# Tokens into the state in matmuls of 128 rows: four token phases side by side, picked out by selection matmuls, and powers of B and C computed 1024 wide

## The reference, cut to what matters

```python
def _s5_mixer(u, a_re, a_im, log_dt, b_re, b_im, c_re, c_im, d, w_glu):
    uf = u.reshape(bsz, L, SSM_GROUPS, SSM_GROUP).astype(f32)       # 256 tokens, 64 groups of 16
    dt = jnp.exp(log_dt)[:, None]
    mag, ang = jnp.exp(a_re * dt), a_im * dt
    lb_re, lb_im = mag * jnp.cos(ang), mag * jnp.sin(ang)            # the eigenvalue lambda
    ...
    bb_re = f_re[..., None] * b_re - f_im[..., None] * b_im          # B, scaled by a complex factor f
    bb_im = f_re[..., None] * b_im + f_im[..., None] * b_re
    bu_re = jnp.einsum('blgp,gnp->blgn', uf, bb_re)                  # tokens into the state
    bu_im = jnp.einsum('blgp,gnp->blgn', uf, bb_im)
    _, _, h_re, h_im = lax.associative_scan(_scan_combine, elems, axis=1)   # h_t = lambda h_(t-1) + bu_t
    y = (jnp.einsum('blgn,gpn->blgp', h_re, c_re)
         - jnp.einsum('blgn,gpn->blgp', h_im, c_im) + d * uf)
    y = jax.nn.gelu(y.reshape(bsz, L, SSM_WIDTH))
    return y * jax.nn.sigmoid(y @ w_glu)
```

## Time and profile before

| | |
|---|---|
| time, median of 3 runs | 3235.52 us (3233.59 to 3236.31) |
| the profiled execution, its own time | 3234.85 us |
| its span in the trace | 3232.8 us |
| TensorE matmul busy | 3206.6 us, 99% |
| TensorE weight load busy | 2650.1 us, 82% |
| VectorE busy | 1868.7 us, 58% |
| ScalarE busy | 1473.2 us, 46% |
| GpSimd busy | 86.3 us, 3% |
| DMA, mean over the span | 183 GB/s |

### The profile page before, as it was taken

How to read it: one execution, slowest core, us unless ns; L and a number is a source line. 1 busy time by engine, 2 the same in 40 slices (tenths; PEclk the granted TensorE clock), 3 DMA queues, 4 the chain that set the end, 5 groups by cost and what they waited for, 6 DMA issues and landing times.

```text
span 3232.8 us, 38841 instructions
## 1 busy us (share of the span) xinstructions
PE 3206.6 (99%) x15914; PEld 2650.1 (82%) x15914; DVE 1868.7 (58%) x2019; ACT 1473.2 (46%) x1786; POOL 86.3 (3%) x84
## 2 busy tenths in 40 slices
PE   8999999999999999999999999999999999999998
PEld 6788888888888888888888888888888888888887
DVE  8676555555555645665555555665566655555556
ACT  7455544444444544454444444454444544444443
POOL 1120000000000000000000000000000000000000
PEclk9999999999999999999999999999999999999999
DMA  6354555555555555655555555645555555555554
GB/s 214 112 151 157 183 185 193 191 188 192 195 184 195 187 186 185 218 179 186 184 191 186 195 183 195 205 164 170 170 169 195 183 192 186 188 189 193 185 194 145
DMA packets 185516, 593.17 MB, mean 183 GB/s; under 512 B 12491, under 2 KB 17276, under 8 KB 184828
## 3 DMA queue, kind: packets, MB, share of 16 engines
q1 hardware_dynamic: 185340, 590.70, 55.5%
HBM read 588.54 MB, written 2.12 MB: 183 GB/s over the span
## 4 chain that ended last, share of the span: by engine, by line
PE 96%; DVE 1%; ACT 1%; issue 1%; DMA 0%; SPq 0%; POOL 0%; POOLq 0%; DVEq 0%; ACTq 0%
PE PS L2378 90%; PE PS L2442 2%; PE PS L2534 1%; PE PS L2399 1%; PE PS L2450 0%; DVE LO L1330 0%; PE PS L2548 0%; PE PS L2554 0%; DMA RAW<-in_w_in 0%; ACT HI L690 0%; ACT CL L852 0%; PE PS L2467 0%; PE PS L2845 0%; DMA RAW<-in_w_out 0%; PE PS L2874 0%
## 5 line engine op out<-in xcount | busy, mean ns | idle before, releaser
L1330 DVE TENSOR_TENSOR LO<-RAW,HI 128x1024 fp32r<-128x1024 f32 (+1 forms) x1104 | 1345.6, 1224 | 1059.0 <-ACT HI L690 1055.8
L690 ACT ACTIVATE HI<-RAW 128x1024 fp32r<-128x1024 f32 (+1 forms) x1104 | 1156.4, 1052 | 1276.7 <-PE PS L2378 1272.1
L2378 PE MATMUL PS<-HI,KPA 128*128 128x512 f32 x5312 | 1470.3, 393 | 3.5 <-ACT HI L690 1.4
L2378 PEld LDWEIGHTS PS<-HI,KPA 128*128 128x128 f32 x5312 | 987.7, 188 | 214.4 <-ACT HI L690 4.6
L2378 PE MATMUL PS<-HI,KPB 128*128 128x512 f32 x3392 | 935.7, 392 | 0.0
L2378 PE MATMUL PS<-LO,KPA 128*128 128x512 f32 x2656 | 824.6, 391 | 1.4 <-DVE LO L1330 1.2
L2378 PEld LDWEIGHTS PS<-HI,KPB 128*128 128x128 f32 x3392 | 629.6, 188 | 126.6
L2378 PEld LDWEIGHTS PS<-LO,KPA 128*128 128x128 f32 x2656 | 499.3, 188 | 110.1 <-DVE LO L1330 4.8
L2378 PE MATMUL PS<-LO,KPB 128*128 128x512 f32 x1696 | 523.4, 390 | 0.0
L2378 PEld LDWEIGHTS PS<-LO,KPB 128*128 128x128 f32 x1696 | 318.3, 188 | 67.3
L750 ACT ACTIVATE KPB<-PS 128x512 fp32r<-128x512 f32 x98 | 58.2, 598 | 174.2 <-PE PS L2442 174.2
(11 more groups left out here) (287 smaller groups left out, 1038.2 us busy)
## 6 DMA issues: line engine op xcount, KB each, us to landing
RAW<-in_w_up SPq DMA_DIRECT2D x128, 1024.0 KB, 5.1
RAW<-in_w_down SPq DMA_DIRECT2D x128, 1024.0 KB, 5.5
RAW<-in_w_qkv SPq DMA_DIRECT2D x48, 1024.0 KB, 5.1
RAW<-in_w_ff_gate SPq DMA_DIRECT2D x88, 512.0 KB, 3.7
RAW<-in_w_ff_up SPq DMA_DIRECT2D x88, 512.0 KB, 4.6
RAW<-in_w_ff_down SPq DMA_DIRECT2D x44, 1024.0 KB, 5.5
RAW<-in_w_in_ab SPq DMA_DIRECT2D x40, 1024.0 KB, 4.9
RAW<-in_w_in SPq DMA_DIRECT2D x16, 1024.0 KB, 5.2
```

Of the source, the lines that this page charges most:

```text
L690: e.activation(HI[plan.slot[s]][:, 0:w], RAW[:, d % NRAW, j, 0:w], ACT.Copy).then_inc(S("hi_made"), 1)
L1330: e.tensor_tensor(LO[h][:, 0:w], RAW[:, d % NRAW, j, 0:w], HI[h][:, 0:w].bitcast(F32), ALU.subtract).then_inc(S("lo_made"), 1)
L2378: ins = e.matmul(PS[:, b + j, 0:cw], l, r[h][:, 512 * j:512 * j + cw], start=(i == 0 and part == 0), stop=(last and part == 2))
```

## The change

The layout of the products into the state is changed, and the order of the preparatory work with it.

1. **Powers.** `product` replaces `times`: real and imaginary part are treated together, 1024 wide, so that a complex product is three instructions (two products, one addition with a negated factor) in place of six of 512. The four powers of B have buffers of their own (B0, BB, P2, P3), and so have those of C; VectorE no longer waits for ScalarE to read one before it makes the next. Two small instructions make the negated factors.
2. **Spreading.** `expand(n)` writes power n of B into XB4, where the four powers lie side by side: 4 x 32 = 128 columns for each j. `turn_b` transposes one j at a time, so BLT[:, part, j, :] has 128 rows: 4 token phases times 32 channels. ScalarE writes B once more to the old XB for the taps (`expand_again`). The turns run later: after u8 to u15 instead of u3 to u11.
3. **Selection.** A constant SEL (128 tokens by 4 phases by 32) is loaded. `u_turn` does its 16 transposes in one go (uT is still needed for out_of_state), and in the next piece 256 matmuls multiply u (128 tokens by 32 channels as weights) with SEL (32 moving columns): every fourth token, phase s to partitions 32s to 32s+31. ScalarE copies the four banks to U4.
4. **Into the state.** `into_state(k)` is 8 matmuls of 128 x 128 weights and 64 moving columns, with nothing accumulated; there are 8 such blocks in place of 16.
5. **Order.** `prep2` is later by two pieces on TensorE, and starts its taps after q4; `spread_c` of the powers 0 to 4 stand elsewhere on ScalarE.

```diff
-    PARTS = [(s, part) for s in (1, 2, 3, 0) for part in range(2)]
+    TURNS = [(part, blk) for part in range(2) for blk in (3, 2, 1, 0)]
+    POWERS = (B0[:, :, :], BB[:, 0:2, :], P2[:, :, :], P3[:, :, :])
...
         def turned_b(n):
-            s, part = PARTS[n]
+            part, blk = TURNS[n]
             q.wait_ge(S("xb_turned"), n + 1)
...
-            for n in range(9):
-                if n < 8:
-                    expand(n)
-                if n:
-                    turned_b(n - 1)
-                if n == 3:
-                    yield
-                    yield
-                yield
-            spread_c(1, 1)
-            yield
-            yield
-            spread_c(2, 2)
-            yield
+            expand(0)
...
+            for n in range(8):
+                turned_b(n)
+                if n == 4:
+                    expand_again()
+                if n == 5:
+                    spread_c(0)
+                if n == 7:
+                    spread_c(1)
+                yield
...
         def prep2():
-            q.wait_ge(S("squared"), NM["ln1"]["squared"] + 4)
-            spread_c(3, 3)
-            yield
             for b in range(4):
                 e.activation(trig_part(0, b), trig_part(1, b), ACT.Abs).then_inc(S("trig_abs"), 1)
+            yield
             q.wait_ge(S("pool_prep"), PP["hp"])
+            spread_c(2)
             for b in range(4):
...
                 yield
+                if b == 0:
+                    spread_c(3)
                 if b == 2:
                     q.wait_ge(S("taps_done"), 2)
-                    spread_c(4, 0)
+                    spread_c(4)
...
+            q.wait_ge(S("u_selected"), 4)
+            for c in range(4):
+                e.activation(U4[:, 8 * c:8 * c + 8, :].rearrange("p a b -> p (a b)"), PS[:, 4 + c, :],
+                             ACT.Copy).then_inc(S("u4_made"), 1)
+            yield
...
-        def times(out, in0, lam):
-            return e.tensor_tensor(small3(out), small3(in0), bcast(lam, 2, 16), ALU.mult)
+        def product(out, src, re, im, extra, last=None):
+            o, x, w = (t.rearrange("p a (j c) -> p a j c", c=16) for t in (out, src, extra))
...
+            e.tensor_tensor(o, x, bcast(bcast(re, 2, 16), 1, 2), ALU.mult)
+            yield
+            then(own(e.tensor_tensor(w, other, bcast(im, 3, 16), ALU.mult)))
+            yield
+            ins = e.tensor_tensor(out, out, extra, ALU.add)
...
         def u_turn():
...
+            q.wait_ge(S("select_loaded"), 16)
+            for c in range(4):
+                q.wait_ge(S("uT_made"), c + 1)
+                for i in range(8):
+                    j = 8 * c + i
+                    for t in range(2):
+                        for s in range(4):
+                            ins = e.matmul(PS[32 * s:32 * s + 32, 4 + c, 64 * i + 32 * t:64 * i + 32 * t + 32],
+                                           u_sb[:, t, 32 * j:32 * j + 32], SEL[:, s, :], start=True, stop=True)
+                ins.then_inc(S("u_selected"), 1)
+            yield
...
-            def into_state(k, i):
-                q.wait_ge(S("uT_made"), 4)
+            def into_state(k):
+                q.wait_ge(S("u4_made"), 4)
                 q.wait_ge(S("bl_made"), 16)
                 if k:
                     q.wait_ge(S(f"ssm{p}_turn"), k)
                 elif p:
                     q.wait_ge(S("taps_read"), 2)
-                q.wait_ge(S(f"ssm{p}_in"), 2 * k + i)
-                for part in range(2):
-                    for s in range(4):
-                        for b in range(2):
-                            rows = slice(32 * (2 * b + i), 32 * (2 * b + i) + 32)
-                            ins = e.matmul(PS[:, ba + b, 128 * part + 64 * i:128 * part + 64 * i + 64],
-                                           BLT[rows, 3 - s, part, 2 * k + p, :], u4(k)[rows, :, s], start=(s == 0), stop=(s == 3))
+                for b in range(2):
+                    for part in range(2):
+                        for i in range(2):
+                            j = 4 * (2 * k + p) + 2 * b + i
+                            ins = e.matmul(PS[:, ba + b, 128 * part + 64 * i:128 * part + 64 * i + 64], BLT[:, part, j, :],
+                                           U4[:, j, :], start=True, stop=True)
                 ins.then_inc(S(f"ssm{p}_in"), 1)
```

More of the change, by code:

```diff
@@ L1474, in prep @@
             q.wait_ge(S("b_loaded"), 32)
-            b0, b1 = B0[:, 0, :], B0[:, 1, :]
-            r = [BB[:, i, :] for i in range(4)]
-            times(b0, r[0], fre)
+            f2, l2, extra = SPR[:, 3:5, :], LAM[:, 1:3, :], BB[:, 2:4, :]
+            yield from product(POWERS[0], BB[:, 0:2, :], fre, f2, extra, "b_powers")
             yield
-            then(own(times(r[2], r[1], fim)))
+            q.wait_ge(S("b_powers"), 1)
+            yield from product(POWERS[1], POWERS[0], lre, l2, extra, "b_powers")
@@ L1495, in prep @@
[L1495 to L1510 removed]
+            q.wait_ge(S("squared"), NM["ln1"]["squared"] + 4)
@@ L1511, in prep @@
+            q.wait_ge(S("turned"), G["xT"].turned0 + 8)
+            for n in (2, 3):
+                q.wait_ge(S("b_powers"), n)
+                yield from product(POWERS[n], POWERS[n - 1], lre, l2, extra, "b_powers")
+            q.wait_ge(S("tau_loaded"), 16)
+            for b in range(4):
+                trig_arguments(b)
                 yield
-                then(own(e.tensor_tensor(c, c, b, ALU.subtract)))
-                then(own(times(a, a, lim)))
-                e.tensor_tensor(d, d, a, ALU.add).then_inc(S("b_powers"), 1)
+            for k in range(1, 4):
+                c = c_power(k)
+                next(c)
+                next(c)
@@ L1515, in prep @@
                 yield
-                for b in (2 * n, 2 * n + 1):
-                    trig_arguments(b)
-                    yield
-            for k in range(1, 4):
-                yield from c_power(k)
+                next(c)
+                yield
         def trig_arguments(b):
@@ L2562, in ssm @@
                     yield
-            for i in range(2):
-                into_state(0, i)
-                yield
+            into_state(0)
+            yield
+            yield
             for k in range(4):
```

188 lines of the change are left out of this document (92 added, 96 removed).

## The result

The changed kernel takes 3249.37 us (median of 5 runs, 3247.86 to 3250.53), the kernel before on the same chip 3233.59 (3233.38 to 3236.31): a ratio of 1.0046, 95% interval 1.0031 to 1.0061. It is slower by 0.46%, where 3237 had been forecast with a range of 3228 to 3243. The profiled execution has a span of 3247.5 us against 3232.8, so 14.7 us are to be found.

A forecast was written before the change was run, and what follows sets the result against it. TensorE was taken as the bound, 96% of the chain of waits. Terms -10.7 (its own work) - 0.7 + 1.0 + 3.9 + 7.4 - 1.6 + 1.6 + 0.8 = +1.7 us on the median 3235.52 gave 3237, range 3228 to 3243.

The forecast's parts named there:

- Into the state: TensorE's blocks into the state: removing the 16 old ones gives -34.0 us, the 64 new matmuls add 14.4 us.
- Selection: TensorE's 256 new matmuls, 512 records at 17.0 ns plus 0.2 us for switching: +8.9 us.
- the line's 11: Lower end for the selection: a line through the 63- and 128-column rows gives 11 ns at 32 columns, 5.8 us.
- Rival 2: Selection at 25 ns a record or nearer 29: 12.8 to 14.8 us instead of 8.7, total 3241 to 3243; 10%.
- A new wait ahead of q0: TensorE waits at q0 for ScalarE's first copy of u: 4.9 us lost against 1.1 before, net +3.9.
- A new wait behind the taps: TensorE's first block of ssm(1) waits for VectorE's copies to KT: +7.4 us (6.5 to 8.5).
- The clock: Half clock: -1.6 us behind the double block, +1.6 behind the taps' wait, +0.8 at q0, 0 after the selection.
- Rival 3: Clock falls three times, also at q0, in the selection (+4) and the step behind it (+1.6): 3243 to 3244; 12%.
- Powers on VectorE: Wider products on VectorE: -0.7 us from the wait in u14, +1.0 in kv (-0.3 to +2.0).
- New waits in glu and attention: Sign of being wrong: new waits in following cycles if scans come late for out_of_state; no size given.
- Rivals 1 and 4: First: wait behind the taps hidden or short, 3228, 13%. Fourth: copies of u not held up at q0, 3232, 5%.

The follow-up runs named there:

- e6: Changed kernel with the selection as 128 products out of uT, each reading 64 contiguous (wrong) tokens: 3237.76 us, ratio 1.0011 to the kernel before.
- e7: Changed kernel with the same selection in four pieces, one PSUM bank after each half step of q: 3242.47 us, ratio 1.0023 to the kernel before.
- e4: Changed kernel with ScalarE's spread of the first power of C moved behind the copies of u and uT: 3243.70 us, ratio 1.0028 to the kernel before.
- e3: Changed kernel with TensorE's taps and VectorE's copies of them one step earlier: 3238.77 us, ratio 1.0013 to the kernel before.
- e8: Changed kernel with a selection of 16 products of 512 columns, plus the edits of e3 and e4: 3227.94 us, ratio 0.9980 to the kernel before.
- e9: e8 with uT laid down phase by phase, so that the selection reads contiguous tokens: 3225.82 us, ratio 0.9971 to the kernel before.
- e12: Changed kernel with the edits of e3 and e4 together, its selection still 256 products: 3232.78 us, ratio 0.9994 to the kernel before.

## Why the prediction was wrong, step by step

- *Into the state*: right. 14.4 us were forecast for the new blocks, 14.2 measured.
- *Selection, 8.9 us (5.8 to 14.8)*: **this step failed.** 14.3 us measured, +5.4, over the 13 us that the prediction had named as a sign of being wrong, with the cause not in the forecast. I took the price of a record from rows of 17.0 ns, in which 64 narrow records stand alone. The records themselves were cheaper, 10 to 16 ns, near the line's 11. But 1024 instructions in a row are four blocks of 256, and they come at one in about 4 us; e6, e7 and the packets of the queue show it. The page of before had the queue, 125 packets, and I did not ask what happens when a block is used up in under 2 us. Rival 2 gave the nearer total, 12.8, for a wrong reason. The 25 ns between starts that the Trainium skill has (TensorE: Matmul & The Clock Gate, section "Wait — 56ns, not 53.3ns?") do not hold for this form: the starts are 10 ns apart at full clock (174 records in 1.71 us).
- *A new wait ahead of q0, +3.9*: right, 4.70 against 0.93, through the chain that I gave; e4 took out one link of it.
- *A new wait behind the taps, +7.4*: right, 7.34; e3 took it away. This and the last were worked out link by link from the order and the pieces of ScalarE and VectorE.
- *The clock, +0.8*: **the second step that failed.** Measured +5.9. I priced a fall at the 1.6 us of one step, half of one at q0, and none at the selection. All three came and cost 1.7, 1.9 and 3.9 us, the last the most, since a block and the step behind it both ran at half. When a short wait brings the clock down stays open, see below. Rival 3 was this one, with 12%; its "+4" in the selection was the wrong place, for a selection that waits for instructions is not slowed much by the clock.
- *Powers on VectorE*: -0.7 in u right; kv +1.5 for +1.0, in its range. The term counted VectorE alone, and 0.6 of it is a wait for ScalarE. The powers by themselves were not tried apart from the layout.
- *New waits in glu and attention*: named at the end as what would be wrong and counted as nothing; +2.3. Rivals 1 and 4, in which a wait would not come, did not happen. The misses all lie on one side: +5.4, +5.1, +2.3 and +0.5, less 0.4 elsewhere, are the 12.9 us between +1.7 and +14.6.

## What to carry to other kernels

Before many narrow matmuls are put in a row, count TensorE's instructions, not only its columns: if 128 records take less than about 3.5 to 4 us and the row is longer than what is held ahead (here the first 174 records never waited), the supply is the bound, and the cure is fewer instructions with more columns, or other work between. Charge an idle piece of TensorE of 4.7 us or more twice, once for itself and once for the work behind it at half clock: in these runs it came behind every wait of 4.7 us ahead of q0 and of 7.3 us behind the taps, with 1.4 to 2.5 us at q0's step and 2.6 (e6) to 3.9 us behind the wait for the taps. A wait of 2.27 us is open: the same wait ahead of q0 was followed by half clock in e4 (q0's step 4.30 us) and by none in e8, e9 and e12 (2.81 to 2.84). A wait worked out link by link from the order of the queues is worth its trouble (4.70 and 7.34 us came out within 0.2), and so is asking which instruction ahead of the releaser could go behind it.
